# Position tables of the first mixer: one table read straight from laid-out input rows, the other as a block of relative shifts; all projection weights issued without a wait

## Time and profile before

| | us |
|---|---|
| median of 3 runs (1284.63 to 1285.61) | 1284.76 |
| the profiled execution, its own time | 1287.93 |
| span of the profiled execution, first to last instruction | 1285.8 |
| busy in the span: PE / PEld / DVE / ACT / POOL | 1038.8 / 461.5 / 280.9 / 129.4 / 41.3 |
| mean granted clock of PE | 0.917 of full |
| SP's wait ahead of unit 2 | 32.0 |
| PE idle between units 1 and 2 of the projection | 10.00 |

### The profile page before, as it was taken

One profiled execution on the slowest core, in us unless ns is written; L12 is line 12 of the kernel. 1 busy time (PEld: TensorE's weight loads), 2 busy tenths in 40 slices (PEclk: granted clock), 3 DMA queues, 4 the chain that ended last, 5 costly groups with the idle time before them and its releaser, 6 DMA issues.

```text
span 1285.8 us, 12306 instructions
## 1 busy us (share of the span) xinstructions
PE 1038.8 (81%) x5118; PEld 461.5 (36%) x5118; DVE 280.9 (22%) x611; ACT 129.4 (10%) x280; POOL 41.3 (3%) x54
## 2 busy tenths in 40 slices
PE   6689999866966677877789899996777687589876
PEld 5456654321311322342257444623213232133422
DVE  2035525210110111110142343431111111011212
ACT  1012410000000000000022011100000000000001
POOL 2630000100000000000000000000000000000000
PEclk9899899987987988989999999999878888899889
DMA  7893275999999999999993314679999999999995
GB/s 238 224 354 160 72 297 233 411 427 428 429 426 430 426 429 426 427 425 426 402 361 131 131 66 182 276 331 426 428 428 427 430 427 429 426 427 428 424 424 213
DMA packets 53261, 447.04 MB, mean 348 GB/s; under 512 B 5382, under 2 KB 7502, under 8 KB 29392
## 3 DMA queue, kind: packets, MB, share of 16 engines
q1 hardware_dynamic: 49328, 438.32, 82.6%
q0 software_dynamic: 3584, 7.36, 2.3%
q10 hardware_dynamic: 288, 0.53, 0.1%
HBM read 445.10 MB, written 3.97 MB: 349 GB/s over the span
## 4 chain that ended last, share of the span: by engine, by line
DMA 52%; PE 38%; SPq 4%; DVE 4%; issue 1%; ACT 1%; POOL 0%; DVEq 0%
PE psum L1330 36%; DMA sb_weights<-moe_w_down 33%; DMA sb_weights<-moe_w_up 15%; SPq L466 3%; DMA sb_weights<-ev_w_in 3%; DMA rpb_rows<-rpb_scratch 1%; SPq L471 1%; DMA sb_x<-x 1%; PE psum L1441 0%; DMA t_scratch<-sb_weights 0%; PE psum L1488 0%; PE psum L1349 0%; ACT sb_hn L596 0%; DVE sb_hT L775 0%; DVE sb_weights L827 0%
## 5 line engine op out<-in xcount | busy, mean ns | idle before, releaser
L1330 PE MATMUL psum<-sb_weights,sb_hT 128*32 128x512 f32 (+2 forms) x2368 | 493.1, 645 | 122.7 <-DMA sb_weights<-moe_w_gate 92.1
L1330 PE MATMUL psum<-sb_weights 128*32 128x512 f32 (+9 forms) x1514 | 318.2, 595 | 67.4 <-DMA sb_weights<-moe_w_down 54.6
L1330 PEld LDWEIGHTS psum<-sb_weights,sb_hT 128*32 128x32 f32 (+2 forms) x2368 | 152.2, 131 | 442.5 <-issue 355.0
L1330 PEld LDWEIGHTS psum<-sb_weights 128*32 128x32 f32 (+6 forms) x1514 | 111.1, 142 | 261.7 <-issue 207.3
L1235 DVE TENSOR_TENSOR sb_x<-sb_x,psum 128x512 f32<-128x512 f32 x88 | 60.3, 687 | 274.2 <-PE psum L1330 274.2
L1330 PE MATMUL psum<-sb_hT,sb_weights 128*128 128x256 f32 (+1 forms) x400 | 92.7, 392 | 2.2 <-DMA sb_weights<-ev_w_in 1.3
L1330 PEld LDWEIGHTS psum<-sb_hT,sb_weights 128*128 128x128 f32 (+1 forms) x400 | 76.8, 194 | 18.2 <-issue 3.2
L1330 PE MATMUL psum<-sb_weights,sb_hn 128*128 128x192 f32 (+1 forms) x384 | 66.8, 336 | 12.1 <-issue 12.1
L1330 PEld LDWEIGHTS psum<-sb_weights,sb_hn 128*128 128x128 f32 x384 | 64.8, 204 | 14.7 <-issue 14.2
L1227 DVE COPY sb_weights<-psum 96x512 f32<-96x512 f32 (+1 forms) x22 | 15.1, 687 | 243.7 <-PE psum L1330 243.7
L1222 DVE TENSOR_TENSOR sb_weights<-sb_weights,psum 96x512 f32<-96x512 f32 (+1 forms) x22 | 15.0, 684 | 171.1 <-PE psum L1330 171.1
(11 more groups left out here) (190 smaller groups left out, 379.7 us busy)
## 6 DMA issues: line engine op xcount, KB each, us to landing
sb_weights<-moe_w_gate SPq DMA_DIRECT2D x64, 2048.0 KB, 24.6
sb_weights<-moe_w_up SPq DMA_DIRECT2D x64, 2048.0 KB, 27.1
sb_weights<-moe_w_down SPq DMA_DIRECT2D x58, 2048.0 KB, 27.3
sb_weights<-moe_w_down SPq DMA_DIRECT2D x12, 1024.0 KB, 18.9
sb_weights<-od_w_in SPq DMA_DIRECT2D x6, 2048.0 KB, 19.8
sb_weights<-ev_w_in SPq DMA_DIRECT2D x5, 2048.0 KB, 32.7
sb_weights<-ev_w_out SPq DMA_DIRECT2D x2, 2048.0 KB, 27.2
sb_weights<-od_w_out SPq DMA_DIRECT2D x2, 2048.0 KB, 7.9
```

The costliest lines, as they stand in the source:

```text
L1330: return nc.tensor.matmul(o, l, r, start=start, stop=stop, skip_group_check=True)
```

## The change

- The host lays out the second table: for each half of the partitions, each head and each of 6 row shifts a row of 128 values, -1e30 with the 31 learned ones in the middle, repeated 64 times (`repeated_rows`, 3.1 MB, an input of the kernel in DRAM). POOL no longer fills, loads, writes or expands it.
- `biasB` is read in two loads, one for each half of the partitions, each 64 x 48 runs of 64 values. It holds 8 heads x 6 shifts x 64 columns; a query tile takes a window of 4 shifts from it (t = 0 from shift 2, t = 1 from shift 0). The mask is added to 3072 values a partition instead of 4096.
- `biasA` is read in one load of 384 values a head and partition; tile t takes a window of 256.
- SP waits for neither POOL's memsets nor the tables: the six units are issued one after the other.
- PE multiplies the T5 table behind the transposes of hn, before the wait for the last piece of hT. ACT copies it to SBUF instead of DVE.
- Lambda's products go to a buffer of their own, without the wait for the scratch writes.

The diff without its blank lines, its declarations of unused semaphores and its list of inputs:

```diff
@@ -110,6 +111,20 @@
     bucket = np.where(rel > 0, half, 0) + np.where(n < exact, n, np.minimum(large, half - 1))
     onehot = (bucket[None, :] == np.arange(T5_BUCKETS)[:, None]).astype(np.float32)
     return c, onehot
+def repeated_rows(rpb):
+    lo = NA_MAX_ROWS - ROWS
+    rows = np.full((P // GRID_W, B_HEADS, SHIFTS, P), MASKED, np.float32)
+    mid = GRID_W - NA_COLS
+    for half in range(P // GRID_W):
+        first = lo + 1 - half
+        rows[half, :, :, mid:mid + 2 * NA_COLS - 1] = np.asarray(rpb)[0, :, first:first + SHIFTS, :]
+    rows = rows.reshape(-1, 1, P)
+    return np.ascontiguousarray(np.broadcast_to(rows, (rows.shape[0], GRID_W, P)))
 def build(nc, A, out):
@@ -182,8 +197,8 @@
         used[0] = 0
         qkT = carve(16 * SEQ).rearrange("p (b t) -> p b t", b=16)
         V0 = carve(TILES * D).rearrange("p (t n) -> p t n", t=TILES)
-        biasA = carve(TILES * A_HEADS * SEQ).rearrange("p (t h k) -> p t h k", t=TILES, h=A_HEADS)
-        biasB = carve(TILES * B_HEADS * SEQ).rearrange("p (t h k) -> p t h k", t=TILES, h=B_HEADS)
+        biasA = carve(A_HEADS * 3 * P).rearrange("p (h c) -> p h c", h=A_HEADS)
+        biasB = carve(B_HEADS * SHIFTS * GRID_W).rearrange("p (h k) -> p h k", h=B_HEADS)
         sc = carve(2 * HALF).rearrange("p (b n) -> p b n", b=2)
         pr = carve(2 * HALF).rearrange("p (b n) -> p b n", b=2)
         prT = carve(2 * HALF).rearrange("p (b n) -> p b n", b=2)
@@ -253,12 +268,7 @@
         t5_dram = nc.dram_tensor("t5_scratch", (A_HEADS, 2 * SEQ), F32, kind="Internal").ap()
-        NDR = 2 * ROWS - 1
-        rpb_dram = nc.dram_tensor("rpb_scratch", (B_HEADS * NDR, P), F32, kind="Internal").ap()
         t5_rows = nc.dram_tensor("t5_rows", (A_HEADS, P, 2 * SEQ), F32, kind="Internal").ap()
-        rpb_rows = nc.dram_tensor("rpb_rows", (B_HEADS * NDR, GRID_W, P), F32, kind="Internal").ap()
         in_full = [sem(f"in_full{c}") for c in range(IN_UNITS)]
@@ -400,8 +409,6 @@
                 w_in = [w_in0, w_in1][layer]
                 for c in range(IN_UNITS):
-                    if layer == 0 and c == 2:
-                        sp.wait_ge(rows_written, 32)
                     if layer == 1:
                         sp.wait_ge(main.used[KINDS[c // 3]], ROUNDS)
                     dst = unit[c].rearrange("p (j n) -> p j n", j=KT)
@@ -473,7 +480,6 @@
             for t in range(TILES):
                 sp.dma_start(x[:, t], A["x"][0, t * P:(t + 1) * P, :]).then_inc(x_loaded[t], 16)
-            sp.wait_ge(gp_done, 2)
             for layer in range(2):
                 mixer_weights(layer)
                 first_round(layer)
@@ -505,45 +511,30 @@
         def _(gp):
             gp.memset(warm, 1.0).then_inc(gp_done, 1)
-            gp.memset(rpbx, MASKED).then_inc(gp_done, 1)
             def load(dst, src):
                 gp.dma_start(dst, src).then_inc(small_loaded, 16)
             gp.dma_start(t5in[0:T5_BUCKETS, :], A["t5_onehot"]).then_inc(t5_loaded, 16)
             gp.dma_start(t5w[0:T5_BUCKETS, :], A["t5_bias"]).then_inc(t5_loaded, 16)
-            gp.wait_ge(gp_done, 2)
-            mid = GRID_W - 1 - (NA_COLS - 1)
-            lo = NA_MAX_ROWS - ROWS
-            gp.dma_start(rpbx[0:B_HEADS * NDR, mid:mid + 2 * NA_COLS - 1],
-                         A["ev_rpb"][0, :, lo:lo + NDR, :]).then_inc(rpb_loaded, 16)
             gp.dma_start(lamrow, A["ev_lambda"].rearrange("l a d -> l (a d)").partition_broadcast(P)
                          ).then_inc(lam_loaded, 16)
             gp.dma_start(subln, A["ev_subln"].rearrange("l d -> d l")).then_inc(lam_loaded, 16)
-            gp.wait_ge(rpb_loaded, 16)
-            gp.dma_start(rpb_dram, rpbx[0:B_HEADS * NDR, :]).then_inc(scratch_written, 16)
             gp.wait_ge(t5_done, 1)
             gp.dma_start(t5_dram, t5rel[0:A_HEADS, :]).then_inc(scratch_written, 16)
-            gp.wait_ge(scratch_written, 32)
-            gp.dma_start(t5_rows, t5_dram.unsqueeze(1).to_broadcast([A_HEADS, P, 2 * SEQ])
-                         ).then_inc(rows_written, 16)
-            gp.dma_start(rpb_rows, rpb_dram.unsqueeze(1).to_broadcast([B_HEADS * NDR, GRID_W, P])
-                         ).then_inc(rows_written, 16)
-            gp.wait_ge(rows_written, 32)
-            for t in range(TILES):
-                gp.dma_start(biasA[:, t], bass.AP(t5_rows.tensor, SEQ - 1 - t * P,
-                                                  [[2 * SEQ - 1, P], [P * 2 * SEQ, A_HEADS], [1, SEQ]])
-                             ).then_inc(biasA_loaded, 16)
-            for t in range(TILES):
-                for rr in range(P // GRID_W):
-                    r = t * (P // GRID_W) + rr
-                    for i in range(ROWS):
-                        src = bass.AP(rpb_rows.tensor, (ROWS - 1 - r + i) * GRID_W * P + GRID_W - 1,
-                                      [[P - 1, GRID_W], [NDR * GRID_W * P, B_HEADS], [1, GRID_W]])
-                        gp.dma_start(biasB[rr * GRID_W:(rr + 1) * GRID_W, t, :, i * GRID_W:(i + 1) * GRID_W],
-                                     src).then_inc(biasB_loaded, 16)
+            gp.wait_ge(scratch_written, 16)
+            gp.dma_start(t5_rows, t5_dram.unsqueeze(1).to_broadcast([A_HEADS, P, 2 * SEQ])).then_inc(rows_written, 16)
+            gp.wait_ge(rows_written, 16)
+            gp.dma_start(biasA, bass.AP(t5_rows.tensor, P - 1, [[2 * SEQ - 1, P], [P * 2 * SEQ, A_HEADS], [1, 3 * P]])
+                         ).then_inc(biasA_loaded, 16)
+            rpb = A["rpb_rows"]
+            for half in range(P // GRID_W):
+                src = bass.AP(rpb.tensor, half * B_HEADS * SHIFTS * GRID_W * P + GRID_W - 1,
+                              [[P - 1, GRID_W], [GRID_W * P, B_HEADS * SHIFTS], [1, GRID_W]])
+                dst = biasB[half * GRID_W:(half + 1) * GRID_W].rearrange("p h (m c) -> p (h m) c", c=GRID_W)
+                gp.dma_start(dst, src).then_inc(biasB_loaded, 16)
             for n, g in ((1, A["norm_ffn"][0]), (2, A["norm_mix"][1]), (3, A["norm_ffn"][1])):
                 load(gain[:, n, :], g.rearrange("(p j) -> p j", j=KT))
             for l in range(2):
@@ -557,9 +548,9 @@
                                  ALU.mult).then_inc(wr_scaled, 1)
             gp.wait_ge(cst_loaded, 16)
-            gp.wait_ge(biasB_loaded, 16 * (SEQ // GRID_W * ROWS))
-            b4 = biasB.rearrange("p t h (i c) -> p (t h i) c", c=GRID_W)
-            gp.tensor_tensor(b4, b4, window.unsqueeze(1).to_broadcast([P, TILES * B_HEADS * ROWS, GRID_W]),
+            gp.wait_ge(biasB_loaded, 16 * (P // GRID_W))
+            b4 = biasB.rearrange("p h (m c) -> p (h m) c", c=GRID_W)
+            gp.tensor_tensor(b4, b4, window.unsqueeze(1).to_broadcast([P, B_HEADS * SHIFTS, GRID_W]),
                              ALU.add).then_inc(biasB_done, 1)
             gp.wait_ge(main.used["gate"], 2)
@@ -599,6 +590,8 @@
                 nc.scalar.activation(rms[:, i:i + 1], rms[:, i:i + 1], ACT.Sqrt).then_inc(rms_done, 1)
             def mixer0():
+                act.wait_ge(t5_psum, 1)
+                nc.scalar.activation(t5rel[0:A_HEADS, :], psum[0:A_HEADS, 7], ACT.Copy).then_inc(t5_done, 1)
                 act.wait_ge(lam_sum, 1)
                 nc.scalar.activation(lamc[:, 0:2], lamc[:, 0:2], ACT.Exp).then_inc(lam_exp, 1)
@@ -793,22 +786,19 @@
                                                 ).then_inc(proj0_done, 1)
-                dve.wait_ge(t5_psum, 1)
-                nc.vector.tensor_copy(t5rel[0:A_HEADS, :], psum[0:A_HEADS, 7]).then_inc(t5_done, 1)
                 for i in range(6):
                     projected(i)
                 dve.wait_ge(lam_loaded, 32)
                 lr = lamrow.rearrange("p (a b d) -> p a b d", a=2, b=2)
-                prod = rpbx.rearrange("p (a d) -> p a d", a=2)
-                dve.wait_ge(scratch_written, 32)
+                prod = lamprod.rearrange("p (a d) -> p a d", a=2)
                 chained(nc.vector.tensor_tensor(prod, lr[:, :, 0, :], lr[:, :, 1, :], ALU.mult))
                 nc.vector.tensor_reduce(lamc[:, 0:2], prod, AX_X, ALU.add).then_inc(lam_sum, 1)
                 dve.wait_ge(lam_exp, 1)
                 chained(nc.vector.tensor_tensor(lamc[:, 2:3], lamc[:, 1:2], lamc[:, 0:1], ALU.subtract))
                 chained(nc.vector.tensor_scalar(lamc[:, 3:4], lamc[:, 2:3], -LAM_INIT, None, ALU.add))
                 chained(nc.vector.tensor_scalar(subln, subln, 1.0 - LAM_INIT, None, ALU.mult))
-                dve.wait_ge(biasA_loaded, 16 * TILES)
+                dve.wait_ge(biasA_loaded, 16)
                 def scores(u):
                     if u == 8:
@@ -820,10 +810,11 @@
                     s = sc[:, u % 2].rearrange("p (m k) -> p m k", m=2)
                     if u < 8:
                         h, t = u // 2, u % 2
-                        bias = biasA[:, t, h:h + 1, :].to_broadcast([P, 2, SEQ])
+                        bias = biasA[:, h:h + 1, (1 - t) * P:(1 - t) * P + SEQ].to_broadcast([P, 2, SEQ])
                     else:
```

(17 more changed lines are left out.)

## The result

| | before | after |
|---|---|---|
| median, us | 1285.18 (4 runs, 1284.63 to 1290.16) | 1274.07 (4 runs, 1269.80 to 1275.70) |
| ratio to before, 95% interval | | 0.9904 [0.9886, 0.9922] |
| the profiled execution, own time / span, us | 1287.93 / 1285.8 | 1272.89 / 1271.1 |

The change saves 12 us by the ratio, 10 to 14.7 by its interval; the medians lie 11.1 us apart. I had forecast 15.3 less, and 1269.5 us; the median is 4.6 us above that and inside the range. The four runs after lie 5.9 us apart, those before 5.5 us (three of them within 1 us): four runs are too few to say that the spread has grown. The two profiled executions differ by 14.7 us of span. That is one draw, and it happens to fit my sum better than the medians do.

What follows compares the result with a forecast made beforehand. Bound where changed: SyncE's queue, holding weight unit 2 for both row tables (32.0 us wait). Terms 14.2 + 0.8 = 15.0 us, plus 0.3 for likelier upside, taken from median 1284.76, gave 1269.5 us; range 1265 to 1276.

Steps and rivals of the forecast that it cites:

- R2: Rival, 0.22: POOL's add lands on the first or second attention step; saves 9.2 to 12.8 us, in the middle 1274.
- Weights issued at once: Projection: units 2 to 5 issued behind unit 1 remove PE's 10.0 and 1.3 us stands and 2.9 us half-clock; saves 14.2 us.
- R1: Rival, 0.25: POOL's add misses DVE altogether, PE's stand shrinks and the clock stays up; saves 17.4 us, giving 1267.4.
- R4: Rival, 0.03: units are issued at once but still come late; unit 3 10 us late saves 5 us, giving 1280.
- First table's matmul: On PE, moved before the wait for DVE's last gain, so the projection starts earlier; saves 0.8 us.
- First table's DMA chain: Scratch write, 13.1 us expansion and load beside the weight stream: lands about 45 us, needed at 63.8, cover 19 us.
- R3: Rival, 0.03: first table arrives late beside the weight stream, DVE and PE stand at the bias; 8 us slower, 1293.
- Second table: Two loads replace the small load, scratch write, expansion and 16 loads; issues off the path, masking add cover 40 us.
- POOL's add beside DVE: Masking add runs 61.5 to 68.1 us, ending as DVE's 128x1 operation comes; same 0.8 us and half-clock stretch, no term.
- The Trainium skill's rule: VectorE instruction with two SBUF inputs and GpSimd instruction reading SBUF exclude each other for the whole instruction; speaks against the change.
- Does it reach the end?: After the projection, through the streamed weights: everything starts earlier by what the projection saved; sum 15.0 us.

Runs made afterwards that it cites:

- Masked rows: Changed kernel with the column mask laid into the second table's rows by the host and POOL's masking add removed; 1269.75 us, ratio 0.9868; run again 1269.21 us, 0.9897.
- loads issued early: Changed kernel with the second table's two loads and the ten small loads issued before POOL's wait for the first table's expansion; masking add kept; 1274.37 us, ratio 0.9902.
- the memset run: Masked rows plus three POOL memsets of 4600 elements a partition into an unused buffer, in the masking add's place; 1273.91 us, ratio 0.9906.

## Why the prediction was right, and where not

The time lies in the range, and not by the forecast's own way: 1274.07 us is R2's "in the middle 1274", and R2's far end is what the range's upper bound was taken from.

- **Weights issued at once, 14.2 us.** Held: no SP wait, no stand, clock 1.00, and 13.90 us for unit 2's matmuls. Masked rows, which keep this part and have no add, are 16.2 and 15.6 us below before, against 17.4 in R1: 1 to 2 us of the sum are not found. Not one of its transfers came late: R4 can go.
- **First table's matmul, 0.8 us.** Held at its place, 0.84, by undoing it; how much of it arrives behind the projection's slower first microseconds is not shown.
- **First table's DMA chain.** Its expansion, for which I kept 13.1 us "since it already ran beside the other table's", took 20.2 from issue to landing under the weight stream and 13.0 with the stream held back (SP's wait put back), by the lists of DMA issues of the changed kernel and of the one with SP's wait put back:

```profile
t_rows<-t_scratch POOLq DMA_DIRECT2D x1, 1024.0 KB, 20.2
...
t_rows<-t_scratch POOLq DMA_DIRECT2D x1, 1024.0 KB, 13.0
```

  The bias landed at 43.35 + 8.4 = 51.8, not 45; cover 12 us instead of 19. R3 stayed away, as the Trainium skill's rule ("DMA: Bandwidth & Descriptors", Queues, rings and completion order) and the trace had it, but the share that the first table kept was smaller than my term.
- **Second table.** Little or nothing of its own: taking SP's wait out of the kernel before, with the add in pieces, gives 13.3 us of the 15.6 of masked rows, without a lighter table. Where SP's wait stays, the lighter table shortens PE's stand from 10.00 to 6.57 us; without the wait it shortens nothing that PE waits for.
- **POOL's add beside DVE: the step that failed.** "I take the same 0.8 us and the same half-clock stretch as before, so no term." The small loads landed at 72.3 and 78.0 us in two executions, not at 60; the add came at 73.6 and 79.3, not at 61.5; and its price was 3 and 9 us, 5.7 by the medians, against the 2.4 that the kernel before pays. Of the 12 us of delay in the first execution 8.7 are the first table's expansion, behind which POOL issued the rest (43.35 instead of 34.7), and 3.5 the loads themselves (29.0 us instead of 25.5). That is R2's mechanism, one to two steps later than R2 had it. Nor was the place that I had taken for likeliest free: the kernel with the loads issued early had the add there, and it held lambda's product for 6.58 us. 15.0 less 5.7, plus the 2.4 that the kernel before already paid, is 11.7; measured were 12 by the ratio and 11.1 by the medians, and 10.5 in the set that the 5.7 comes from, which is the 1.2 us by which masked rows stay short of R1 there.
- **The Trainium skill's rule** ("SBUF — State Buffer", Who interferes with whom) was the most useful sentence of the prediction, and I had given it a chance of 0.22 where the traces then show a meeting in every kernel with a whole add but one (SP's wait put back). It also says that `tensor_scalar` can take the shared ports in its faster modes; the memset run agrees for the 128x256 TENSOR_SCALAR (2.12 against 0.35 us), which I had not put in the sum.
- **Does it reach the end?** Held: 14.71 us at unit 3's projection, 14.64 at the first chained weight DMA, 14.7 of span.

The best kernel that was run is masked rows: 1269.75 and 1269.21 us, 5.7 us below the changed kernel of its set, with the smaller spread there.

## What to carry to other kernels

A long GpSimd operation on SBUF is a lottery ticket for VectorE: an operation that it meets with two SBUF inputs can be held for nearly the whole of it (5 to 9 us in four of six meetings here), and TensorE's clock can fall behind the stand. Cut it into pieces, or have the host do it, before tuning where it lands. When undoing a part of a change moves the time by nothing, look where the next cost landed: here a wait worth 7 to 9 us looked free, since putting it back moved the add to where nothing met it.

## What the runs showed of the hardware

- In four of the six kernels in which a DVE operation met the whole add it was held for most of it: 6.75 us beside an add of 6.69, 8.91 beside 8.85, 6.58 beside 6.66, 5.03 beside 6.64; in the other two it took 0.97 and 1.78. In the first two of these four POOL's router scalings ran just ahead and had already held the operation before (0.73 and 0.72 instead of 0.35); POOL's next instruction then started before DVE's next. That this lines them up is my reading of the rows, and was not tried by itself; in the first profile of the changed kernel the scalings held two operations (0.82 and 0.78 us) and the add did not hold the next one for its length.
- The add itself took 6.86 us in that profile, against 6.64 to 6.69 in the others, and started at 73.64, while DVE's operation with two SBUF inputs ran until 73.97: a sign that POOL can be the one that waits, from one execution.
- Small loads on POOL's queue took 18.5 and 24.7 us from the last issue to landing behind 1.6 MB in 256-byte runs and beside the weight stream, 15.5 with the weights held back; behind the 2.1 MB of the kernel before it was 13.3 us with SP's wait and 29.4 without.
- A load of 3,072 runs of 256 bytes cost POOL 1.37 us of issue, against 0.68 for one of 512: twice the time for six times the runs.
